# The bias products and their addition moved behind the first weight unit in the second block's projection

## The reference, cut to what matters

```python
h = rms_norm(x, norm_gain[layer])
proj = h @ w_in[layer]                                   # 512 x 1024 times 1024 x 8448
qa, ka, va, qb, kb, vb, ga, gb, mg = jnp.split(proj, split_idx, axis=-1)
...
rel = mi[None, :] - blk - qi[:, None]
bias = bias_table[t5_bucket(rel * stride)]               # (blk, 3*blk, heads)
...
valid = (kpos >= 0) & (kpos < L) & (jnp.abs(kpos - qpos) <= half_window)
logits = jnp.where(valid, scores + bias, NEG_INF)
```

## Time and profile before

| | |
|---|---|
| time before, median of 3 runs | 1476.79 us (1476.45 to 1480.57) |
| the profiled execution's own time | 1477.63 us |
| its span in the profile | 1475.9 us |
| PE busy over the span | 1288.1 us (87%) |
| DVE, ACT, POOL busy | 564.3 us, 479.1 us, 173.1 us |
| granted TensorE clock, mean | 0.933 |

### The profile page before, as it was taken

One profiled execution on the slowest core, in us unless ns is written; L12 is line 12 of the kernel. 1 busy time (PEld: TensorE's weight loads), 2 busy tenths in 40 slices (PEclk: granted clock), 3 DMA queues, 4 the chain that ended last, 5 costly groups with the idle time before them and its releaser, 6 DMA issues. The chain is left out here.

```text
span 1475.9 us, 24366 instructions
## 1 busy us (share of the span) xinstructions
PE 1288.1 (87%) x10299; PEld 998.4 (68%) x10299; DVE 564.3 (38%) x1010; ACT 479.1 (32%) x806; POOL 173.1 (12%) x219
## 2 busy tenths in 40 slices
PE   5999797579986949998883699999989989899988
PEld 4888753269966735654442698888877767666668
DVE  3331132765653132322223513344438753522222
ACT  4222266612134221111112424555545533111120
POOL 4000032010004012322211001122200000000030
PEclk9999899789997969998987799999999999999989
DMA  4332000000017559999996346233152026113011
GB/s 144 114 100 72 1 0 0 14 3 4 4 59 287 201 193 367 386 390 394 390 405 228 90 152 135 77 100 96 58 73 71 30 91 226 57 57 114 0 58 58
DMA packets 92488, 195.53 MB, mean 132 GB/s; under 512 B 9510, under 2 KB 73084, under 8 KB 79452
## 3 DMA queue, kind: packets, MB, share of 16 engines
q1 hardware_dynamic: 86604, 183.48, 36.5%
q0 software_dynamic: 5200, 8.40, 1.8%
q10 hardware_dynamic: 576, 2.10, 0.4%
HBM read 184.74 MB, written 16.81 MB: 137 GB/s over the span
## 5 line engine op out<-in xcount | busy, mean ns | idle before, releaser
L1768 PE MATMUL hidden_ps<-w_gate,gathered_t 128*64 128x256 f32 x432 | 116.4, 430 | 24.1 <-DMA w_up<-exp_w_up_dram 23.3
L1768 PE MATMUL hidden_ps<-w_up,gathered_t 128*64 128x256 f32 x432 | 116.4, 430 | 0.0
L1768 PEld LDWEIGHTS hidden_ps<-w_gate,gathered_t 128*64 128x64 f32 x432 | 64.8, 156 | 62.6 <-issue 36.8
L1333 PE MATMUL wo_ps<-w_out_high,wo_x_high 128*128 128x256 f32 x256 | 75.2, 294 | 19.2 <-POOL wo_x_low L1374 19.2
L414 PE MATMUL proj_ps<-block_in_high,w_in_low 128*128 128x512 f32 x232 | 90.5, 390 | 0.0
L414 PE MATMUL proj_ps<-block_in_low,w_in_high 128*128 128x512 f32 x232 | 90.5, 390 | 0.0
L414 PE MATMUL proj_ps<-block_in_high,w_in_high 128*128 128x512 f32 x232 | 90.4, 390 | 0.0
L462 DVE TENSOR_TENSOR w_in_low<-w_in_raw,w_in_high 128x2048 fp32r<-128x2048 f32 x20 | 45.8, 2292 | 116.4 <-ACT w_in_high L454 116.4
L414 PE MATMUL gate_ps<-block_in_high,gate_w_high 128*128 128x512 f32 x192 | 79.8, 416 | 11.3 <-DVE gate_w_low L462 11.3
L414 PE MATMUL gate_ps<-block_in_low,gate_w_high 128*128 128x512 f32 x192 | 76.5, 398 | 0.0
L414 PE MATMUL gate_ps<-block_in_high,gate_w_low 128*128 128x512 f32 x192 | 76.3, 397 | 0.0
(11 more groups left out here) (456 smaller groups left out, 3147.2 us busy)
## 6 DMA issues: line engine op xcount, KB each, us to landing
w_gate<-exp_w_gate_dram SPq DMA_DIRECT2D x27, 1024.0 KB
w_up<-exp_w_up_dram SPq DMA_DIRECT2D x27, 1024.0 KB
w_down<-exp_w_down_dram SPq DMA_DIRECT2D x27, 1024.0 KB
w_in_raw<-w_in_dram SPq DMA_DIRECT2D x20, 1024.0 KB, 5.7
slot_scratch_and_keys<-w_in_dram SPq DMA_DIRECT2D x14, 1024.0 KB, 5.3
vb<-w_in_dram SPq DMA_DIRECT2D x6, 1024.0 KB, 5.6
gate_w_raw_odd<-w_in_dram SPq DMA_DIRECT2D x6, 1024.0 KB, 5.9
slot_scratch_and_keys<-exp_w_gate_dram SPq DMA_DIRECT2D x5, 1024.0 KB
```

Source lines behind the costliest of these rows:

```text
L1333: m = pe.matmul(banks[n % nb][:, 0:UNIT], x[a][k][:, c * P:(c + 1) * P], wts.parts(u, k, slice(0, UNIT))[b], start=(k == 0 and a + b == 0) ...
L1768: x = pe.matmul(g_bank[e % 2][a * CAP:(a + 1) * CAP, 0:DE], xT[e % 2][:, k, :], w[:, k, :], start=(k == 0), stop=(k == KC - 1))
```

## The change

`bias.pick` moves on PE from in front of the products of unit 0 to behind all of them, before job 2. `bias.add_windows` moves on DVE from behind the third low part of the input to behind the low part of unit 1. DVE's wait for the stores moves to the first job that writes into `qa`. SP's program is not touched.

```diff
                 feats.turn(pe, 0)
                 feats.turn(pe, 1)
-                bias.pick(pe)
                 wts.wait(pe, 0)
                 for k in range(KC):
...
                 for c in (1, 3):
                     split_product(pe, bank[c // 2][:, UNIT:2 * UNIT], lambda k: [p[:, k, c * P:(c + 1) * P] for p in hT],
                                   lambda k: wts.parts(0, k, slice(0, UNIT)), KC).then_inc(ready, 1)
+                bias.pick(pe)
                 for n, (u, kind, x, dst, gain, perm) in enumerate(jobs):
...
                 wts.split_low(dve, 0)
                 for k in range(KC):
                     feats.low(dve, k)
-                    if k == 2:
-                        bias.add_windows(dve)
                 wts.split_low(dve, 1)
-                dve.wait_ge(bias.stored, 64)
+                bias.add_windows(dve)
                 for m, (u, *_) in enumerate(jobs):
                     if last_job.get(u - 1) == m - 1:
                         wts.split_low(dve, u + 1)
                     n = m - 1
                     if n not in normed:
                         continue
+                    if n == normed[0]:
+                        dve.wait_ge(bias.stored, 64)
```

## The result

| | before | after |
|---|---|---|
| median of 8 runs each | 1476.62 us (1474.24 to 1480.57) | 1484.38 us (1481.91 to 1485.45) |
| ratio, 95% interval | | 1.0051 [1.0039, 1.0062] |
| the profiled execution's own time | 1477.63 us | 1484.37 us |
| its span | 1475.9 us | 1482.7 us |

What follows compares the result with a forecast made beforehand. The projection was taken to be bound by PE, its stream full from 842 to 1080 us. Start -0.1, passes 1.8, standstill 4.9 and clock 1.1 summed to +7.7 us, so 1484.5 us, range 1478.4 to 1487.5.

Steps and rivals of the forecast that it cites:

- The start gains nothing: Start of the stage on PE and DVE: without bias products and addition, a gain of 0.1 us (0 to 0.25).
- The passes: PE's stream between unit 0 and unit 1: four small float32 passes of the bias products, paid in full, 1.8 us.
- The stores and the load: SP's queue: first store 16.7 us later, at 850.3; unit 3's load lands 22.8 us after it, at 873.1.
- The first rival: SP's stores run at an ordinary load's pace, unit 3 is in time, only passes paid: +1.7 us, 1478.5; chance 0.18.
- The estimate from the page: The four stores on SP: 1 MB in an estimated 4.5 us at 8 of 16 DMA engines, so the first rival would hold.
- The standstill: PE before unit 3: waits 4.9 us for the low part, because unit 3's load lands late.
- The clock: PE behind the standstill: clock falls to half for about 4.1 us of new work, taken as 1.1 us.
- The sum: Whole kernel: -0.1 + 1.8 + 4.9 + 1.1 = +7.7 us, giving 1484.5 us.
- The second rival: Projection on PE: more than one unit late, or the clock falls twice, also behind the passes; some 1488; chance 0.09.
- The third: Start on PE: without small passes the clock stays up, 1.2 us back; 1483.3 with stall, 1477.3 without (chance 0.03).

Runs made afterwards that it cites:

- filled standstill: Changed kernel plus 20 thrown-away 512-column products on PE before the wait for unit 3; 1483.96 us, ratio to the kernel before 1.0052.
- stores behind unit 3: Changed kernel with SP issuing the load of unit 3 before the four bias stores; 1477.09 us, ratio to the kernel before 1.0005.
- passes twice: Run stores behind unit 3, with the two bias products made twice, so eight passes on PE; 1479.29 us, ratio to the kernel before 1.0016.

## Why the prediction was right, by its own steps

**The start gains nothing.** Predicted -0.1 us, measured 0. PE's first product of unit 0 stands 827.64 - 821.35 = 6.29 us after the stage's first instruction before, and 826.98 - 820.69 = 6.29 after. The passes begin at 847.11 - 820.69 = 26.4 us, where 847.76 - 821.35 = 26.4 was due. The bias products had indeed cost nothing there.

**The passes.** Predicted 1.8 us; 848.92 - 847.11 = 1.81. With the stores out of the way the stage was 1.9 us longer. Doubled, they also brought the clock down.

**The stores and the load.** Predicted 16.7 us later and a landing 22.8 us after the first store; 16.8 (849.74 - 820.69 against 833.63 - 821.35) and 22.9. The price carried over: the same five transfers follow each other in the same order. The load's issue did start 1 us sooner after the first store (9.9 us against 10.9), and that gave nothing, as assumed. The first rival, stores quick in new surroundings, fell with the 9.88 us. The estimate from the page "DMA: Bandwidth & Descriptors" of the Trainium skill (Specifications), 4.5 us for the four, fell with it.

**The standstill.** Predicted 4.9 us; the row has 4.85. To the first product of unit 3 the stage took 870.80 - 821.35 = 49.45 us before and 877.07 - 820.69 = 56.38 after, 6.9 more, of which 1.8 are the passes and 5.1 the standstill with the tail of the last product. Moving the stores made it vanish, moving only the addition made it 2.14 us.

**The clock.** Here the prediction was right in kind and half in size: 1.1 us predicted, 9.2 - 6.9 = 2.3 paid, 2.2 given back when the standstill was filled. The mis-sized term has two faults. It took the loss from 7 against 11 matmuls in stretches of 1 us. Such a count takes in the products that are already under way at the stretch's edge; the changed kernel's stretches of products alone show the same two counts:

```profile
842.00:843.00 1.00, 1.00 (x11) 1.00 (x10) 1.00 (x1) 0.00 (x0) 0.00 (x0) 1.00 0.00 0
878.00:879.00 1.00, 1.00 (x7) 1.00 (x6) 0.00 (x0) 0.00 (x0) 0.00 (x0) 0.50 0.83 119
```

From start to start the pace is 0.12 against 0.215 us, a loss of 0.44 of the time and not 4/11, or 0.36. And it took 1.1 us, below the 1.5 that its own rows gave for 4.1 us of work at the half clock; that work was 5.0 us here, and 5.0 x 0.44 = 2.2.

**The sum.** -0.1 + 1.8 + 4.9 + 1.1 = 7.7 was predicted and 0 + 1.8 + 5.1 + 2.3 = 9.2 is in the stage. The medians moved by 7.8. That the forecast of 1484.5 met the 1484.38 so closely is therefore partly luck: it was 1.5 us too low in the stage, and it gave nothing to the rest of the kernel, which took 2.4 us less in the profile. Of that, 1.8 us lie behind the stage and go with the clock there, as shown with the result; 0.7 us ahead of it stay open. The prediction had no term for a clock that differs in stages that the change doesn't touch. The rest took between 1200.5 and 1204.6 us over all these profiles, in kernels that are alike there.

**The rivals.** The second rival's fall of the clock behind the passes did not come in the changed kernel, but did with eight of them, and cost 1.5 us. The third, that the start would be faster without the passes, was wrong as put: the clock fell with the passes (at 828.0), and fell without them (at 827.5). It stayed only where full-size products filled the wait.

## What to carry to other kernels

Work that is moved later on a compute engine also delays everything that stands behind the wait for it in another engine's queue. Here an addition 16.8 us later was free on DVE, and made a load late that has nothing to do with it, on SP. So put a slow transfer that nobody needs soon behind the loads that set the pace, and count the slack of the next load from its landing, not from when it is used. Work that looks like a cost at the start of a stage may stand in the one gap where it is free; and price a standstill of TensorE with the slow products behind it, in the stage. In the whole time such a price can be lost in what the clock does later: the filled standstill won 2.2 us in its stage and nothing that the total shows.

## What the runs showed of the hardware

- Four stores of 256 KB that read from 8 partitions each take SP 9.9 us to issue (0.69 us the shortest, 4.15 us the longest), and a load behind them 2.9 to 3.8 us of issue against 0.37. Issued by GpSimd they take 0.63 to 0.70 us each. They hold a load in the same queue for 6 to 7 us (11.9 and 13.0 against 5.8 to landing), and one from another queue for 4 to 5 us (10.0).
- The clock fell after a standstill of 2.1 us in one run, after 4.85 us in another, and after eight small passes of 3.5 us with PE never idle. With four of them in the same place it did not fall.
- The same code up to the passes had the clock rise at 824.2 and fall again at 827.6 in one execution (stores behind unit 3), and stay at half until 829.7 in another (passes twice). Both reached the passes 26.4 to 26.5 us into the stage.
- Two products of 512 columns, ahead of the small passes at the start, went with a clock that stayed up where it had fallen without them, and a stage 1.0 us shorter; three did so too, with 0.8 us. Each is one execution.
